# Two attention heads side by side on TensorE, and sums of squares moved from TensorE to VectorE, in a two-block kernel

## The reference, cut to what matters

```
# end of the first block
gate = sigmoid(rmsnorm(x, g_ple) @ w_ple_gate)
x = x + gate * (p @ w_ple_proj)
x = rmsnorm(x, g_final)
# second block
h = rmsnorm(x, norm_mix_pre);  proj = h @ w_in        # 4608 columns
conv_in, q, k, v, g_conv, g_att = split(proj)
u = glu(conv_in); u = causal_depthwise_conv(u, 31 taps); u = silu(layernorm(u))
z = q k^T / 8                    # per head, 256 x 256, two blocks of queries
log_1m = where(mask, log_sigmoid(-z), 0)
a = where(mask, exp(log_sigmoid(z) + (reverse cumsum of log_1m, exclusive)), 0)
att = a @ v                      # per head, 64 columns
merged = sigmoid(g_conv) * (u @ w_conv_branch + b) + sigmoid(g_att) * (att @ w_att_branch)
```

## Time and profile before

| | |
|---|---|
| median of 3 runs | 964.51 us (963.71 to 965.91) |
| profiled execution | 964.45 us, of which 962.7 us from the first to the last instruction |
| TensorE matmul busy | 935.1 us, 97% |
| VectorE busy | 498.7 us, 52% |
| ScalarE busy | 330.4 us, 34% |
| GpSimd busy | 39.2 us |
| memory traffic | 289.45 MB, 301 GB/s |
| granted TensorE clock | 0.997 of full speed |

### The profile page before, as it was taken

How to read it: one execution, slowest core, us unless ns; L and a number is a source line. 1 busy time by engine, 2 the same in 40 slices (tenths; PEclk the granted TensorE clock), 3 DMA queues, 4 the chain that set the end, 5 groups by cost and what they waited for, 6 DMA issues and landing times.

```text
span 962.7 us, 14239 instructions
## 1 busy us (share of the span) xinstructions
PE 935.1 (97%) x5914; PEld 660.7 (69%) x5914; DVE 498.7 (52%) x869; ACT 330.4 (34%) x527; POOL 39.2 (4%) x39
## 2 busy tenths in 40 slices
PE   7999999999999899999999899999999999999997
PEld 6997734444444444443344499988889999999886
DVE  7784613222212322222132397997788987776642
ACT  6832211001101010100011367556456755644541
POOL 1000000000000000000000000222320000000000
PEclk9999999999999999999999999999999999999999
DMA  9987799999999999999999974442334424555301
GB/s 348 403 368 325 296 396 430 428 433 429 432 428 432 427 430 430 431 432 428 431 429 419 428 302 165 176 175 88 135 129 175 176 110 176 208 211 195 132 1 44
DMA packets 28982, 289.45 MB, mean 301 GB/s; under 512 B 3057, under 2 KB 6385, under 8 KB 12401
## 3 DMA queue, kind: packets, MB, share of 16 engines
q1 hardware_dynamic: 28192, 286.91, 72.9%
q10 hardware_dynamic: 720, 1.57, 0.4%
HBM read 287.43 MB, written 1.05 MB: 300 GB/s over the span
## 4 chain that ended last, share of the span: by engine, by line
PE 82%; DVE 6%; SPq 5%; ACT 3%; DMA 2%; issue 2%; POOL 0%; DVEq 0%; ACTq 0%
PE ps L279 81%; SPq L2244 5%; DVE wl L275 3%; DMA ring<-in_w_pg 2%; ACT wh L268 1%; PE ps L1063 1%; DMA arena<-in_xT 0%; DVE arena L1549 0%; ACT arena L1848 0%; DVE arena L1889 0%; DVE arena L1960 0%; DVE mg_l L1896 0%; DVE mix_l L606 0%; ACT arena L1851 0%; DVE arena L593 0%
## 5 line engine op out<-in xcount | busy, mean ns | idle before, releaser
L279 PE MATMUL ps<-ring,arena 128*64 128x512 f32 x1216 | 339.2, 597 | 4.8 <-issue 4.7
L275 DVE TENSOR_TENSOR wl<-ring,wh 128x1024 fp32r<-128x1024 f32 x150 | 180.5, 1235 | 49.4 <-ACT wh L268 49.3
L279 PEld LDWEIGHTS ps<-ring,arena 128*64 128x64 f32 x1216 | 109.5, 137 | 122.1 <-issue 120.3
L268 ACT ACTIVATE wh<-ring 128x1024 fp32r<-128x1024 f32 x150 | 151.7, 1051 | 48.5 <-PE ps L279 34.3
L279 PE MATMUL ps<-arena 128*64 128x512 f32 (+4 forms) x448 | 166.7, 523 | 0.9 <-DMA ring<-in_moe 0.4
L279 PEld LDWEIGHTS ps<-arena 128*64 128x64 f32 (+2 forms) x448 | 58.6, 144 | 89.6 <-issue 82.8
L1168 DVE SCALAR_TENSOR_TENSOR arena<-ps,arena 128x512 f32<-128x512 f32 x16 | 12.0, 751 | 202.6 <-PE ps L279 202.6
L279 PE MATMUL ps<-up_h,wh 128*128 128x256 f32 x352 | 85.5, 281 | 0.7 <-ACT up_h L1949 0.7
L279 PE MATMUL ps<-up_l,wh 128*128 128x256 f32 x352 | 82.1, 280 | 0.0
L1238 ACT ACTIVATE y_h<-ps 128x512 fp32r<-128x512 f32 x32 | 19.0, 596 | 151.9 <-PE ps L279 151.9
L279 PEld LDWEIGHTS ps<-up_h,wh 128*128 128x128 f32 x352 | 66.3, 188 | 0.9 <-issue 0.9
(11 more groups left out here) (275 smaller groups left out, 1487.6 us busy)
## 6 DMA issues: line engine op xcount, KB each, us to landing
ring<-in_moe SPq DMA_DIRECT2D x69, 2048.0 KB, 22.5
arena<-in_moe SPq DMA_DIRECT2D x17, 2048.0 KB, 22.4
ring<-in_w_in SPq DMA_DIRECT2D x12, 2048.0 KB, 10.6
ring<-in_w_up SPq DMA_DIRECT2D x11, 2048.0 KB, 7.6
ring<-in_moe SPq DMA_DIRECT2D x24, 512.0 KB, 15.1
ring<-in_w_dn SPq DMA_DIRECT2D x5, 2048.0 KB, 7.8
ring<-in_w_out SPq DMA_DIRECT2D x4, 2048.0 KB, 16.0
arena<-in_moe SPq DMA_DIRECT2D x8, 512.0 KB, 14.6
```

Source lines behind the costliest of these rows:

```text
L268: e.activation(wh(i), raw_piece(i), ACT.Copy).then_inc(*hi.up(i))
L275: e.tensor_tensor(wl(i), raw_piece(i), wh(i), SUB).then_inc(*lo.up(i))
L279: return e.matmul(o, l, r, start=first, stop=final, skip_group_check=True)
```

## The change

- In `mixer_pe` the last three sums of squares come before the first product and no longer in its middle.
- In `ple` the sum of squares is added up on VectorE in three steps (`added`: 1024, 512 and 256 columns), and TensorE has one float32 matmul in place of eight. VectorE's `split_lo` of pieces 8 to 12 moves behind the stage's own work.
- In `in2` the four first products (`four_late`) use all of wh first and wl last. Of the two chains of sums the plain one becomes `added` and one matmul, made after piece 1 into `ps[3]` and copied by ScalarE; its root moves to `merge_act`. The weighted chain stays.
- `scores` and `values` make two heads in one call, with each head's matmul of a kind next to the other's.
- `gate` scales two results at a time, 512 columns; the order of taps' sum in `merge_pe` is 3, 0, 1, 2, with each waited for alone.

```diff
+        def four_late(e, outs, name, n, xh, xl, ready, at):
+            i0 = n_piece[(name, n), 0]
+            for j in range(4):
+                e.wait_ge(*hi.at(i0 + j))
+            for c in range(8):
+                e.wait_ge(*ready.at(c))
+                for j in range(4):
+                    mm(e, outs[j], wh(i0 + j)[:, c, :], xh[:, c, :], c == 0, False)
+                    mm(e, outs[j], wh(i0 + j)[:, c, :], xl[:, c, :], False, False)
+                at(e, c)
+            for j in range(4):
+                e.wait_ge(*lo.at(i0 + j))
+                for c in range(8):
+                    k = mm(e, outs[j], wl(i0 + j)[:, c, :], xh[:, c, :], False, c == 7)
+                k.then_inc(*proj.up(name, n, j))
...
-            squares((1, 0, 3, 2, 5))
-            three(e, ps[3][:, 0:256], "in1", 0, 0, XGH, XGL, xg, between=lambda: squares((7, 4, 6)))
+            squares((1, 0, 3, 2, 5, 7, 4, 6))
+            three(e, ps[3][:, 0:256], "in1", 0, 0, XGH, XGL, xg)
...
-        def sums(e, c):
+        def sum_gained(e, c):
             e.wait_ge(*sq4.at(c))
-            a = mm(e, ps[6][:, 0:256], inv1024, SQ[:, c, :], c == 0, c == 7)
-            b = mm(e, ps[7][:, 0:256], gsq[:, c:c + 1].to_broadcast([128, 128]), SQ[:, c, :], c == 0, c == 7)
+            k = mm(e, ps[7][:, 0:256], gsq[:, c:c + 1].to_broadcast([128, 128]), SQ[:, c, :], c == 0, c == 7)
...
+        def added(e, out, ready, steps):
+            e.wait_ge(*ready.at(7))
+            e.tensor_tensor(SQ[:, 0:4, :], SQ[:, 0:4, :], SQ[:, 4:8, :], ADD).then_inc(*steps.up("four"))
+            e.wait_ge(*steps.at("four"))
+            e.tensor_tensor(SQ[:, 0:2, :], SQ[:, 0:2, :], SQ[:, 2:4, :], ADD).then_inc(*steps.up("two"))
+            e.wait_ge(*steps.at("two"))
+            e.tensor_tensor(out, SQ[:, 0, :], SQ[:, 1, :], ADD).then_inc(*steps.up("all"))
...
-            four(e, [ps[j][:, 0:256] for j in range(4)], "pgate", 0, XPH, XPL, ple, first=ple_h, at=norm3)
+            four(e, [ps[j][:, 0:256] for j in range(4)], "pgate", 0, XPH, XPL, ple, first=ple_h)
+            e.wait_ge(*sum3.at("all"))
+            mm(e, ps[7][:, 0:256], inv1024, SQ[:, 0, :], True, True).then_inc(*means.up("r3"))
...
-            split_lo(e, FIRST + 8)
+            added(e, SQ[:, 0, :], sq3, sum3)
+            split_lo(e, FIRST + 6)
...
             for j in range(8):
-                if j == 1:
+                if j == 0:
                     recip(e, "r3", RB[:, 0, :])
                     e.wait_ge(*recips.at("r3"))
-                if j >= 1:
+                else:
                     scale(j - 1)
+                split_lo(e, FIRST + min(6 + j, 8))
...
-                split_lo(e, FIRST + (8, 8, 9, 10, 12, 12, 12, 12)[j])
...
-            split_lo(e, FIRST + 16)
+            split_lo(e, FIRST + 13)
...
+            for h, b in zip(hs, bk):
+                r = 64 * (h % 2)
+                mm(e, b[:, 0:256], KT[r:r + 64, j, 0:128], QT[r:r + 64, j, :], True, False)
+            for h, b in zip(hs, bk):
+                mm(e, b[:, 0:128], IDR[:, :], NMR[:, :], False, False)
+            for h, b in zip(hs, bk):
+                r = 64 * (h % 2)
+                mm(e, b[:, 256:384], KT[r:r + 64, j, 128:256], QT[r:r + 64, j, 128:256], False, False)
+            for h, b in zip(hs, bk):
+                mm(e, b[:, 256:384], IDR[:, :], NMR[:, :], False, False).then_inc(*s_sc.up(h))
...
+            for h in hs:
+                r = 64 * (h % 2)
+                mm(e, b[r:r + 64, 0:256], VT[:, 0, h * 64:h * 64 + 64], AB[h % 4][:, 0:256], True, False)
+            for h in hs:
+                r = 64 * (h % 2)
+                mm(e, b[r:r + 64, 128:256], VT[:, 1, h * 64:h * 64 + 64], AB[h % 4][:, 256:384], False,
+                   True).then_inc(*s_val.up(h))
...
+            e.wait_ge(*scaled.at(3))
+            four_late(e, [ps[j][:, 0:256] for j in range(4)], "in2", 0, H5H, H5L, h5, norms)
...
+            e.wait_ge(*gs_in.at(3))
+            e.wait_ge(*sum4.at("all"))
+            mm(e, ps[3][:, 0:256], inv1024, SUM4, True, True).then_inc(*means.up("r4"))
...
-                if j in (1, 2):
-                    scores(e, j - 1)
+                if j == 1:
+                    scores(e, 0)
...
             suffix(e, 1)
-            scores(e, 2)
+            scores(e, 1)
             wide(e, ps[1][:, :], "in2", 4, 1, H5H, H5L)
-            scores(e, 3)
...
+            e.wait_ge(*means.at("r4"))
+            e.activation(R4, ps[3][:, 0:256], ACT.Copy).then_inc(*r4m.up(0))
             for j in range(8):
                 split_hi(e, IN2 + 15 + j)
...
+            split_lo(e, IN2 + 8)
+            added(e, SUM4, sq4, sum4)
             split_lo(e, IN2 + 10)
...
-                three(e, ps[j % 2][:, 0:256], "in2", 5 + n, j, H5H, H5L)
-                if g in (1, 3, 5, 7):
-                    scores(e, 4 + g // 2)
+                three(e, ps[g // 2 % 2][:, g % 2 * 256:g % 2 * 256 + 256], "in2", 5 + n, j, H5H, H5L)
+                if g in (1, 5):
+                    scores(e, 2 + g // 4)
                 if g in (0, 2, 4, 6, 8, 10):
                     suffix(e, 2 + g // 2)
-                if g in (0, 1, 2, 4, 6, 8, 10, 12):
-                    values(e, (0, 1, 2, 4, 6, 8, 10, 12).index(g))
+                if g in (1, 4, 8, 12):
+                    values(e, (1, 4, 8, 12).index(g))
...
-            mean(e, ps[0][:, 0:256], CA, inv512, [tap_v.at(j, 30) for j in range(3)] + [tap_p.at(30)], "mu")
+            for c in (3, 0, 1, 2):
+                e.wait_ge(*(tap_v.at(c, 30) if c < 3 else tap_p.at(30)))
+                k = mm(e, ps[0][:, 0:256], inv512, CA[:, c, :], c == 3, c == 2)
```

More of the change, by code:

```diff
@@ L1377, in build @@
         scaled = sig("scaled", range(8))
+        sum3 = sig("sum3", ["four", "two", "all"])
+        sum4 = sig("sum4", ["four", "two", "all"])
+        SUM4 = RB[:, 1, :]
         gate = sig("gate", range(8))
@@ L1535, in build @@
         at_l = h5.then(range(4))
-        sg_in = sig("sg_in", range(16))
+        sg_in = sig("sg_in", range(8))
         chunks = [(n, j) for n in range(4) for j in range(4)]
@@ L1559, in taps_act, with scores @@
             del todo["act"][:n]
-        def scores(e, h):
-            b, r, j = 2 + h % 4, 64 * (h % 2), h // 2
+        def scores(e, j):
+            hs = (2 * j, 2 * j + 1)
+            bk = [ps[2 + h % 4] for h in hs]
             e.wait_ge(*k_.at(j))
-            if h == 0:
+            if j == 0:
                 for x in range(2):
                     e.wait_ge(*masks.at(x))
-            elif h == 2:
+            elif j == 1:
                 e.wait_ge(*rc.at(0))
[L1570 to L1575, removed]
+            else:
+                e.wait_ge(*s_at.at(hs[0] - 4))
+                e.wait_ge(*s_at.at(hs[1] - 4))
+            for h, b in zip(hs, bk):
[8 more added lines that the diff above has]
+                mm(e, b[:, 256:384], IDR[:, :], NMR[:, :], False, False).then_inc(*s_sc.up(h))
         def suffix(e, h):
@@ L1624, in norms @@
                     for x in range(5):
[L1625 to L1628, removed]
-            four(e, [ps[j][:, 0:256] for j in range(4)], "in2", 0, H5H, H5L, h5, at=norms)
+                        sum_gained(e, x)
+                if c >= 5:
+                    sum_gained(e, c)
+            e.wait_ge(*scaled.at(3))
+            four_late(e, [ps[j][:, 0:256] for j in range(4)], "in2", 0, H5H, H5L, h5, norms)
             for j in range(4):
-                e.wait_ge(*(scaled.at(4 + j) if j < 2 else roots.at("r4" if j == 2 else "r45")))
+                e.wait_ge(*(scaled.at(4 + j) if j < 3 else roots.at("r45")))
                 three(e, ps[4 + j][:, 0:256], "in2", 1, j, H5H, H5L)
+            e.wait_ge(*gs_in.at(3))
+            e.wait_ge(*sum4.at("all"))
+            mm(e, ps[3][:, 0:256], inv1024, SUM4, True, True).then_inc(*means.up("r4"))
             for j in range(4):
-                e.wait_ge(*gs_in.at(j))
+                e.wait_ge(*(gs_in.at(j) if j < 3 else r4m.at(0)))
                 three(e, ps[j][:, 0:256], "in2", 2, j, H5H, H5L)
@@ L1654, in in2_act @@
             root(e, "r45", R45, ps[7][:, 0:256], squared=1)
-            for was in emptied(*last_in(8)):
-                e.wait_ge(*was)
-            e.wait_ge(*means.at("r4"))
-            root(e, "r4", R4, ps[6][:, 0:256])
             e.preload_act_table_set("sigmoid_and_others")
@@ L1756, in att_dve @@
             for g in range(16):
-                if g:
-                    gate(g - 1)
-                split_lo(e, IN2 + 20 + g + 7)
+                if g and g % 2 == 0:
+                    gate(g // 2 - 1)
+                split_lo(e, IN2 + 20 + min(g, 14) + 7)
                 if g in (3, 6, 10, 14):
@@ L1766, in att_dve @@
                     softplus_dve(e, 3 + g // 2)
-            gate(15)
+            gate(7)
             taps_dve(e, 1000)
@@ L1836, in merge_act @@
             e.preload_act_table_set("sqrt_and_others")
+            root(e, "r4", R4, R4)
             e.wait_ge(*proj.at("in2", 8, 3))
```

48 lines of the change are left out of this document (25 added, 23 removed).

## The result

The changed kernel takes 950.67 us (median of four, 950.59 to 950.91), the kernel before beside it 965.21 us; the ratio is 0.984, with a 95% interval of 0.983 to 0.985. The gain, 14.5 us, is small beside the whole (1.6%), but far more than the fraction of a microsecond by which the four executions differ. The forecast was 952.3. The profiled execution took 950.72 us, with 949.0 us from the first instruction to the last at a granted clock of 0.995; TensorE's matmuls are busy for 921.4 us of it, VectorE for 501.4.

The account below looks back on a forecast made before the run. TensorE was taken to bound the kernel from 550 us on. Its 14.5 us of savings less waits of 1.2 + 1.4 + 1.1 is 10.8, plus 1.4 from a shorter tail: 12.2 us less, 952.3 us; range 949.6 to 957.2.

Parts of the forecast that it names:

- sums: Sums of squares in ple and in2: 7 x 0.41 and 7 x 0.43 us less TensorE work, 2.9 and 3.0 us.
- the order of the scores: In att, two heads' scores interleaved in one call take 1.78 us, not 3.04; 5.0 us gained for four pairs.
- values: In att, column halves overlap, so a pair's second head is nearly free: 0.9 us a pair, 3.6 in all.
- the 32-row records: Four products on 32 rows by 64 columns in 0.65 us, not 0.86: the ground for full overlap in scores.
- The start: The mixer's sums and products change places within 10.61 to 15.33 us: costed at nothing.
- waits of 1.2 + 1.4 + 1.1: TensorE's waits for VectorE: in `four_late` 1.2 us, before the first scores 1.4, before the first suffix 1.1.
- the round of q: VectorE's four rounds of q take 3.23 us each against TensorE's 2.82, so the first pair's k is ready at 620.3.
- no new waits: Rival: VectorE's parts and k come in time, 15.9 us less, 948.6 us; chance 0.05.
- Partial overlap: Rival: the scores' row halves run one after the other, or scores and values save only a pass: 954.5 us; chance 0.14.
- no overlap: Rival: neither row nor column halves overlap in att, only entries and sums are saved: 957 us; chance 0.04.
- VectorE is the bound: Rival: 4.8 us more VectorE work between 558 and 607 us, lag in q and k growing 5 us: 957; chance 0.10.
- Slower, by the clock: Rival: longer waits in the middle drop the clock, 2.6 us each; six drops give 967 us; chance 0.03.

Follow-up runs that it names:

- control: The changed kernel run once more without any edit, the table's second column of measurements: 951.02 us (950.34 to 952.94).
- the rounded kernel: Changed kernel with all sums of squares on TensorE as rounded products, `added` gone, two new tiles moving the activations by 544 bytes: 943.92 us.
- the last one: Changed kernel with rounded sums, activations shifted by two tiles, and GpSimd's taps moved out of the rounds of q: 940.49 us, ratio 0.974 to the kernel before.

## Why the prediction was right, and where it was off

The mechanism held in each part that was undone. TensorE's time between 550 us and the convolution's mean was the program's time, and the terms came out by their own undoing: sums 5.9 forecast, 5.3 measured; the order of the scores 1.26 a pair, 1.32 measured; values 0.9 a pair, 0.96 measured. The order of products inside `four_late`, the wider steps of `gate` and the later root were not undone by themselves; the forecast had them at next to nothing, and no run tells. The row halves of the array, of which the trace of before had shown no pair, overlap in full (1.70 us for a pair of heads, 1.78 forecast, 2.42 without the overlap); the choice of the 32-row records as nearest row was right. The start cost nothing.

Off were the waits. Points on the way, in us from ple's first matmul:

| | forecast | changed kernel | the same again |
|---|---|---|---|
| ple's products end | +23.6 | +23.0 | +23.0 |
| VectorE enters q | +56.7 | +55.4 | +55.3 |
| first k ready | +70.0 | +68.0 | +68.9 |
| first suffix | +78.9 | +76.7 | +77.3 |
| att's last product ends | +152.5 | +149.8 | +150.3 |
| subtraction, L1925 | +154.5 | +151.7 | +152.2 |

The step that failed is "waits of 1.2 + 1.4 + 1.1": the profiled execution has 0.26 + 0.57 in `four_late`, none at the first scores, and 0.7 at the first suffix (0.52 of it idle, the rest lost behind it), 1.5 us for 3.7. That is 2.2 of the 2.8 us by which the touched stages beat the forecast; 0.3 is the pair of scores, and 0.3 I leave open. It failed for two reasons. VectorE's parts ended 0.8 us earlier than by the rounds of 1.77 us taken from before, and it came to q 1.3 us early. And the round of q, 3.23 us by the trace of before, is no constant: 3.05 in one execution and 3.30 in the next, by how GpSimd's taps fall on it, 2.60 without them. The wait for k is thus anything from nothing to 1.05 us in six executions whose program is the same from ple up to there. The changed kernel's own profile is one of the two without it, and that is luck; the 1.4 us are too much in all six, but a term of 1.0 would have been a fair one. The 1.0 us that the experts' end took back, and 0.3 behind, brought the total from 2.8 to 1.5 us off.

The range has a slip of its own: half of the waits gone is 1.85 us, which gives 950.4 and not 949.6. The measured 950.67 lies above either, but near the edge.

Of the rivals, "no new waits" (948.6) was nearer to this stage than the waits that I summed: 2.2 of 3.7 were not there. Partial overlap and no overlap are refuted by the records. "VectorE is the bound" is half alive. The control's chain goes through VectorE up to 627 us; but taking GpSimd's taps away moved the subtraction by only 0 to 0.6 us, taking 4.7 us of additions off VectorE at TensorE's cost lost 5.3 us, and the lag stays under the 5 us it would have needed. "Slower, by the clock" did not come here, but its mechanism is real: in three experiments the clock fell to 1.2 GHz behind a wait in this stretch, which cost 1.7 to 3.4 us each time.

The order of the sum in the tail was right: TensorE's last product, one matmul of the mean behind the last tap, and the subtraction 2.0 us later (149.8 to 151.7).

## What to carry to other kernels

When TensorE bounds a stretch, count its passes and entries, since those of scores and values came out within 0.1 us a pair (0.2 for the values against the other profile) and the sums within 0.6 of 5.9; but price a wait for another engine as a range, from the rounds of several executions, because two nearly equal lines meet there. Two heads on the two halves of the rows or columns need only stand in one call; the order within the call mattered for the scores, where full-array mask products stand between, and not for the values. Before crediting an edit with a gain in stages that it didn't touch, move the tiles alone: declaring two unused ones gained 3.9 us.

## What I had not expected of the hardware

- Rounded products of 256 columns follow each other at 117 to 120 ns with the activations where they were, and at 113 to 114 ns in stretches of tens of microseconds with them 544 bytes further on, both at a granted clock of 1.00. In `down`, 512 columns come at 233.3 ns in the changed kernel and at 228.9 in the rounded kernel and the last one, though there the 512 columns are those of `wh` and `wl`, which haven't moved, and the activations are the stationary side; with the place alone they come at 233.4. What switches a stretch from one to the other within one execution is open.
- The clock falls behind some waits and not behind others of the same length: after 1.04 us in the kernel with serial scores and not after 1.04 us in the control or 1.05 with the values in eight calls; after 2.01 us with the place shifted alone and not after 1.84 us in the rounded kernel. It was at 1.2 GHz for 3.4 us in one case and for 6.8 us in another. What decides isn't settled.
- The second head's values start 0.01 us behind the first head's in both orders of the program that were run (8 records in 0.80 and 0.81 us).
